# Three groups of transposes moved from TensorE to VectorE and swapped loads, and a silu as one ScalarE instruction, in a three-layer float32 model

## The reference, cut to what matters

```python
# even layer, short-convolution branch
y_a = sc_b * causal_depthwise_conv(sc_c * sc_v, sc_conv_w)
y_a = y_a * jax.nn.silu(sc_z)
# even layer, scan branch
xbc = jax.nn.silu(causal_depthwise_conv(ssd_xbc, ssd_conv_w) + ssd_conv_b)
xs, bm, cm = _split(xbc, (SSD_WIDTH, SSD_GROUPS * SSD_STATE, SSD_GROUPS * SSD_STATE))
y_b = ssd_chunked(xs, dt, a, bm, cm) + xs * ssd_d[:, None]
y_b = y_b.reshape(b_, l_, SSD_WIDTH) * jax.nn.silu(ssd_z)      # then a norm per group
return x + jnp.concatenate([y_a, y_b, y_m], axis=-1) @ w_out
# odd layer
y_c = causal_block_attention(q_full, k_full, v) * jax.nn.silu(z_c)
return x + jnp.concatenate([y_c, y_m], axis=-1) @ w_out
```

## Time and profile before

| what | us |
|---|---|
| median of 3 runs | 2671.36 |
| lowest and highest of them | 2669.19 and 2673.0 |
| the profiled execution's own time | 2667.36 |
| its span, first to last instruction | 2665.8 |
| TensorE busy in it | 2646.0 |
| VectorE busy | 1554.9 |
| ScalarE busy | 1348.1 |

### The profile page before, as it was taken

One profiled execution on the slowest core, in us unless ns is written; L12 is line 12 of the kernel. 1 busy time (PEld: TensorE's weight loads), 2 busy tenths in 40 slices (PEclk: granted clock), 3 DMA queues, 4 the chain that ended last, 5 costly groups with the idle time before them and its releaser, 6 DMA issues.

```text
span 2665.8 us, 35952 instructions
## 1 busy us (share of the span) xinstructions
PE 2646.0 (99%) x12095; PEld 2199.0 (82%) x12095; DVE 1554.9 (58%) x1827; ACT 1348.1 (51%) x1787; POOL 336.2 (13%) x519
## 2 busy tenths in 40 slices
PE   9999999999999999999999999999999999999998
PEld 7888888888888888888888878888888889888887
DVE  6444456667555555555454564446777765457864
ACT  6544455654444444444444554446565445555443
POOL 2100032211110000000000111001110010123300
PEclk9999999999999999999999999999999999999999
DMA  8866676678876767666666877666666777687664
GB/s 313 307 227 216 215 235 222 204 242 271 243 231 211 221 211 225 209 220 229 215 219 218 257 228 233 209 204 238 224 227 227 242 243 226 222 269 218 182 216 162
DMA packets 171057, 608.53 MB, mean 228 GB/s; under 512 B 22880, under 2 KB 22928, under 8 KB 170192
## 3 DMA queue, kind: packets, MB, share of 16 engines
q1 hardware_dynamic: 133632, 485.03, 55.3%
q0 software_dynamic: 36608, 121.07, 14.9%
q10 hardware_dynamic: 720, 1.11, 0.1%
HBM read 557.79 MB, written 50.90 MB: 228 GB/s over the span
## 4 chain that ended last, share of the span: by engine, by line
PE 92%; DVE 2%; issue 2%; DMA 2%; ACT 1%; POOL 0%; POOLq 0%; SPq 0%; ACTq 0%; DVEq 0%
PE acc L802 58%; PE acc L808 29%; DVE w_lo L1848 1%; DMA d_x<-tile 1%; DMA raw<-stream 1%; DMA r_b<-d_x 1%; PE turn L1098 1%; ACT w_hi L1285 0%; PE ps_s L1228 0%; PE ps_s L1229 0%; POOL r_b L558 0%; PE ps_y L893 0%; PE ps_y L1003 0%; PE ps_s L880 0%; PE ps_s L988 0%
## 5 line engine op out<-in xcount | busy, mean ns | idle before, releaser
L1848 DVE TENSOR_TENSOR w_lo<-raw,w_hi 128x1024 fp32r<-128x1024 f32 x919 | 1117.7, 1223 | 883.0 <-ACT w_hi L1285 876.3
L1285 ACT ACTIVATE w_hi<-raw 128x1024 fp32r<-128x1024 f32 x919 | 963.9, 1059 | 899.8 <-PE acc L808 821.9
L802 PE MATMUL acc<-w_hi,x_t_hi 128*128 128x512 f32 (+1 forms) x2400 | 950.5, 396 | 3.8 <-DVE x_t_lo L1897 3.1
L802 PE MATMUL acc<-w_hi,x_t_lo 128*128 128x512 f32 (+1 forms) x2400 | 933.5, 389 | 0.0
L808 PE MATMUL acc<-w_lo,x_t_hi 128*128 128x512 f32 (+1 forms) x2400 | 640.8, 389 | 0.2 <-DVE w_lo L1848 0.2
L802 PEld LDWEIGHTS acc<-w_hi,x_t_hi 128*128 128x128 f32 x2400 | 451.2, 188 | 96.2 <-DVE x_t_lo L1897 3.5
L808 PEld LDWEIGHTS acc<-w_lo,x_t_hi 128*128 128x128 f32 x2400 | 451.1, 188 | 93.1 <-DVE w_lo L1848 0.6
L802 PEld LDWEIGHTS acc<-w_hi,x_t_lo 128*128 128x128 f32 x2400 | 451.3, 188 | 90.5 <-issue 1.9
L802 PE MATMUL acc<-w_hi,ff_t_hi 128*128 128x512 f32 x352 | 136.9, 389 | 0.0
L802 PE MATMUL acc<-w_hi,ff_t_lo 128*128 128x512 f32 x352 | 136.9, 389 | 0.0
L808 PE MATMUL acc<-w_lo,ff_t_hi 128*128 128x512 f32 x352 | 94.1, 389 | 0.0
(11 more groups left out here) (398 smaller groups left out, 2691.9 us busy)
## 6 DMA issues: line engine op xcount, KB each, us to landing
raw<-stream SPq DMA_DIRECT2D x919, 512.0 KB, 4.3
d_in<-tile POOLq DMA_DIRECT2D x20, 512.0 KB, 3.8
d_ev<-tile POOLq DMA_DIRECT2D x20, 512.0 KB, 4.9
d_x<-tile POOLq DMA_DIRECT2D x16, 512.0 KB, 4.2
r_b<-d_x POOLq DMA_DIRECT2D x64, 128.0 KB, 5.9
xin<-d_x POOLq DMA_DIRECT2D x16, 512.0 KB, 8.6
d_h<-tile POOLq DMA_DIRECT2D x14, 512.0 KB, 5.0
h_b<-d_h POOLq DMA_DIRECT2D x56, 128.0 KB, 4.8
```

Of the source, the lines that this page charges most:

```text
L802: nc.tensor.matmul(out, src[x][:, chunk + c, t * P:(t + 1) * P], w_hi[:, s, w], start=first and c == 0 and x == 0, stop=False)
L1285: nc.scalar.activation(w_hi[:, u.slot, :], raw[:, u.slot, :], ACT.Copy).then_inc(hi_ready, 1)
L1848: nc.vector.tensor_tensor(w_lo[:, s, :], raw[:, s, :], w_hi[:, s, :].bitcast(F32), ALU.subtract).then_inc(lo_ready, 1)
```

## The change

RES_AT of the stage "gate" goes from (8, 9, 10) to (7, 8, 9). The scan's 768 columns are loaded by four swapped loads into `u_b` and transposed by one VectorE instruction into `u_t` in SBUF, at position 15 of the group before; the convolution reads `u_t`. The silu of the convolution and that of the gate become one ScalarE instruction each, both at position 4, and VectorE's multiplies go. The short convolution's halves are loaded swapped, and its two operands are transposed by VectorE; the halves stand 9 positions apart, and TensorE waits for the second before unit 22. Tiles 0 to 2 of the latent output are written to `d_h` and read back swapped through ScalarE's DMA queue, transposed by VectorE and split by `high_blocks` and `low_blocks`; tile 3 stays as it was. The columns are put in order on the host. GpSimd's loads of `xin` for the last residual wait for the third of these tiles, since they share its memory.

```diff
-RES_AT = {"mix": (5, 6, 8), "ffo": (5, 6, 7), "gate": (8, 9, 10)}
+RES_AT = {"mix": (5, 6, 8), "ffo": (5, 6, 7), "gate": (7, 8, 9)}
```

GpSimd's queue, the loads for the scan and the short convolution, and the wait ahead of the last residual's loads:

```diff
         def load_u(g):
-            pool.dma_start(u_in[:, :, 0:512], ev_v[:, :, bass.ds(g.times(512, 1024), 512)]).then_inc(s_u, 16)
-            for m in range(2):
-                pool.dma_start(u_in[:, :, 512 + m * P:640 + m * P],
-                               ev_v[:, :, bass.ds(g.times(P, 3072 + 512 * m), P)]).then_inc(s_u, 16)
+            for b in range(P // SQ):
+                w = 1024 + 768 * g.k + 6 * SQ * b
+                pool.dma_start(u_b[b * SQ:(b + 1) * SQ, :, :],
+                               d_ev[:, w:w + 6 * SQ].rearrange("(a j) n -> j a n", j=SQ)).then_inc(s_u, 16)
...
-            for t in range(TH):
-                pool.dma_start(sc_in[:, t, :, :].rearrange("p a n -> p (a n)"),
-                               ev_v[:, t, 6144 + 2048 * j:6144 + 2048 * (j + 1)]).then_inc(c_in, 16)
+            for b in range(P // SQ):
+                w = 6144 + 2048 * j + NBW * b
+                pool.dma_start(sc_in[b * SQ:(b + 1) * SQ, :, :, :].rearrange("p a k n -> p a (k n)"),
+                               d_ev[:, w:w + NBW].rearrange("(a j) n -> j a n", j=SQ)).then_inc(c_in, 16)
...
+        pool.wait_ge(turn_lo, 2 * (TURN["oy"] + 3) + 2)
         for b in range(4):
             free = [] if b < 2 else [(sums_out, B0["oout"] + b + 1)]
             load_tile(halves(d_x4), At(b), b % 2, free)
```

TensorE, scan (the transposes at position 0):

```diff
-            if p == 0:
-                pe.wait_ge(s_u, n.times(48, 48))
+            if p == 7:
                 pe.wait_ge(dt_v, 7)
                 pe.wait_ge(s_yb, n.times(1, 1))
-                for c in range(6):
-                    bank = (turn[0], turn[1], ps_s)[c // 2]
-                    for t in range(TH):
-                        mm = nc.tensor.transpose(bank[:, (c % 2 * TH + t) * P:(c % 2 * TH + t + 1) * P],
-                                                 u_in[:, t, c * P:(c + 1) * P], ident[:, :])
-                mm.then_inc(s_ut, 1)
-            if p == 7:
```

TensorE, beside eout (its function `short`, with 2 x 16 transposes, is removed):

```diff
-            if q == 20:
-                pe.wait_ge(c_lo, 2)
+            if q in (20, 22):
+                pe.wait_ge(c_lo, q // 2 - 9)
```

TensorE, latent output:

```diff
-            for n in range(4):
+            for n in range(3, 4):
                 for h in range(2):
                     if p == GATED + 8 * n + 2 * h:
```

ScalarE, scan:

```diff
             if p == 4:
                 act.wait_ge(s_conv, n.times(3, 3))
-                nc.scalar.activation(th[:, :], cv[:, :, :].rearrange("p c t -> p (c t)"), ACT.Tanh)\
-                    .then_inc(s_th, 1)
-            if p == 5:
+                c_ = cv[:, :, :].rearrange("p c t -> p (c t)")
+                nc.scalar.activation(c_, c_, ACT.Silu, scale=2.0).then_inc(s_silu, 1)
                 act.wait_ge(s_z, n.times(16, 16))
-                nc.scalar.activation(zth[:, :, :], zt[:, :, :], ACT.Tanh, scale=0.5).then_inc(s_zth, 1)
+                nc.scalar.activation(zt[:, :, :], zt[:, :, :], ACT.Silu).then_inc(s_zs, 1)
```

ScalarE, latent output (tile 3 keeps the steps of before):

```diff
+            for n in range(3):
+                if p == GATED + 8 * n - 1:
+                    act.wait_ge(l_tile, n + 1)
+                    act.dma_start(halves(d_h), ybuf[:, :, n * NBW:(n + 1) * NBW]).then_inc(heads_in, 16)
+                if p == GATED + 8 * n + 1:
+                    act.wait_ge(heads_in, OUT_MOVES * n + 16)
+                    if n:
+                        act.wait_ge(turned, 2 * (TURN["oy"] + n))
+                    for b in range(P // SQ):
+                        act.dma_start(o_b[b * SQ:(b + 1) * SQ, :, :],
+                                      d_h[:, b * P:(b + 1) * P].rearrange("(a j) n -> j a n", j=SQ)).then_inc(heads_in, 16)
+                if p == GATED + 8 * n + 5:
+                    high_blocks(TURN["oy"] + n, o_r, o_t, n)
```

VectorE, scan (the two multiplies at positions 5 and 6 are removed; this is called at position 15 of the stage ez and of groups 0 to 2):

```diff
+        def turn_u(g):
+            dve.wait_ge(s_u, 64 * (g + 1))
+            dve.wait_ge(s_conv, 3 * g)
+            nc.vector.transpose(u_t[:, :, :].rearrange("p c (a i) -> p c a i", i=SQ),
+                                u_b[:, :, :].rearrange("p a (c i) -> p c a i", i=SQ)).then_inc(s_ut, 1)
```

VectorE, short convolution (its steps stand at positions 9j + 4, 6, 7, 8, 9 and 11, where they stood at 7j + 4, 6, 8 and 11):

```diff
+            for at, src, dst, ready, done in ((6, 1, sc_u, c_u, c_ut), (7, 0, sc_w, c_w, c_wt)):
+                if k == 9 * j + at:
+                    dve.wait_ge(ready, j + 1)
+                    dve.wait_ge(c_y, j)
+                    nc.vector.transpose(dst[:, :, :].rearrange("p c (a i) -> p c a i", i=SQ),
+                                        sc_in[:, :, src, :].rearrange("p a (c i) -> p c a i", i=SQ)).then_inc(done, 1)
```

VectorE, latent output:

```diff
+                if n < 3 and p == GATED + 8 * n + 4:
+                    turn_blocks(TURN["oy"] + n, OUT_MOVES * (n + 1), o_b, o_r, heads_in)
+                if n < 3 and p == GATED + 8 * n + 7:
+                    low_blocks(TURN["oy"] + n, o_r, o_t, n)
```

More of the change, by code:

```diff
@@ L244, in program @@
     lat_junk = place("lat_junk", [P, 2560], F32, XT + 3 * K)
+    o_b = place("o_b", [P, TOK // SQ, P], F32, END + 8 * K)
+    o_r = place("o_r", [P, 4 * TOK], F32, END + 12 * K)
     zgt = place("zgt", [P, TH, NBW], F32, WD + 64 * K)
@@ L1122, in _ @@
             pair_of("sc", 2 * g, 0, 0, 8, x3_t, 0, lambda p: sc_beside(p, g))
-        def short(p, j):
-            if p == 8 + 7 * j:
-                if j:
-                    pe.wait_ge(c_y, j)
-                else:
-                    pe.wait_ge(turn_lo, 2 * TURN["x4"] + 2)
-                pe.wait_ge(c_u, j + 1)
-                pe.wait_ge(c_w, j + 1)
-                for src, banks, s_ in ((sc_in[:, :, 1, :], turn, c_ut), (sc_in[:, :, 0, :], (ps_s, ps_y), c_wt)):
-                    for h in range(2):
-                        for c in range(2):
-                            for t in range(TH):
-                                mm = nc.tensor.transpose(
-                                    banks[h][:, (c * TH + t) * P:(c * TH + t + 1) * P],
-                                    src[:, t, (2 * h + c) * P:(2 * h + c + 1) * P], ident[:, :])
-                        mm.then_inc(s_, 1)
         for q, (b, k) in enumerate(EOUT_ORDER):
@@ L1145, in _ @@
             turn_group(q, 3)
-            for j in range(2):
-                short(q, j)
             if q == 6:
@@ L2383, in sc_beside @@
                 low_group(p, g - 1)
+            if p == 15 and g < 3:
+                turn_u(g + 1)
         for g in range(4):
@@ L2598, in latent_heads @@
                     for t in range(TH):
-                        last = nc.vector.tensor_scalar(ybuf[:, t, J * P:(J + 1) * P],
-                                                       ps_y[:, t * P:(t + 1) * P], sums[:, 4 + t:5 + t], None,
-                                                       ALU.mult)
+                        y_ = ybuf[:, t, J // 4 * NBW:(J // 4 + 1) * NBW].rearrange("p (b c i) -> p b c i", b=4, i=SQ)
+                        y_ = y_[:, :, J % 4, :] if J < 12 else ybuf[:, t, J * P:(J + 1) * P]
+                        z_ = ps_y[:, t * P:(t + 1) * P]
+                        last = nc.vector.tensor_scalar(y_, z_.rearrange("p (b i) -> p b i", i=SQ) if J < 12 else z_,
+                                                       sums[:, 4 + t:5 + t], None, ALU.mult)
                     last.then_inc(l_y, 1)
@@ L2702 @@
     w0 = a["w_in0_2"]
-    ein = np.concatenate([w0[:, 9248:EVW], w0[:, 6144:9216], w0[:, 4096:6144]], axis=1)
+    xbc = np.concatenate([w0[:, 6144:8192].reshape(D, 4, 4, 4, SQ)] + [
+        w0[:, at:at + 512].reshape(D, 4, 1, 4, SQ) for at in (8192, 8704)], axis=2).transpose(0, 1, 3, 2, 4)
+    ein = np.concatenate([w0[:, 9248:EVW], xbc.reshape(D, -1), w0[:, 4096:6144]], axis=1)
     dt = w0[:, 9216:9248].reshape(16, P, 32).transpose(1, 0, 2).reshape(1, P, -1)
-    short = np.concatenate([w0[:, 1024 * m + NBW * j:1024 * m + NBW * (j + 1)]
-                            for j in range(2) for m in range(4)], axis=1)
+    short = w0[:, :4096].reshape(D, 4, 2, 4, 4, SQ).transpose(0, 2, 4, 1, 3, 5).reshape(D, -1)
     out0 = np.concatenate([a["w_out0_2"][1024:], a["w_out0_2"][:1024]])
```

73 lines of the change are left out of this document (33 added, 40 removed).

## The result

The changed kernel takes 2672.18 us (median of 20 runs, 2667.70 to 2676.46), the kernel before takes 2668.11 us in the same session (20 runs, 2665.05 to 2673.00). The ratio is 1.0013, 95% interval 1.0007 to 1.0019. That is a slowdown of about 0.1%, inside what I had called no change, and 17.5 us above the forecast of 2654.7. The forecast stood on a median of 3 runs, 2671.36, which is 3.2 us above that of the 20: measured on the change alone, 16.7 us were to be won and 4.1 were lost.

The account below looks back on a forecast made before the run. TensorE bounds the kernel, busy 2646.0 of 2665.8 us. Gains 5.40 + 3.54 + 2.76 + 5.01 = 16.7 us take 2667.36 to 2650.7, plus 4.0 for the median gives 2654.7 us; range 2650 to 2663.

Parts of the forecast that it names:

- the cover: Whole change: added work fits into idle time and leads on the other engines and transfers, without making TensorE wait.
- Gate: Opening of ein: TensorE's wait for the residual's low part goes, winning 5.01 us, with 0.7 us in hand.
- Latent output: Four transposes fewer at each of six places win 2.76 us; the added stores, loads and transposes cost nothing.
- Scan: Twelve transposes fewer per group, 1.35 us each group, win 5.40 us over four groups.
- So it has a little less to do than before: VectorE in a scan group: gains a transpose of 1.86 us, loses a 1.75 us multiply and another of 1024 columns.
- 2.6 us are left: Scan position 4: ScalarE's split of unit 7 ends at 1910.8, TensorE wants it at 1913.4.
- Rival (4): Scan position 4: ScalarE late behind two table loads and two silu, each group waits 5.0 us, 2674.7 us; chance 0.03.
- The table loads cost no time: Scan: two loads a group, 2.56 us, fit into ScalarE's 3.72 us idle before the silu.
- a late load would first eat the ring's lead: Scan operands: even a late swapped load would first use the lead of the splits queued on VectorE; landing takes 5.9 us.
- Short convolution: Sixteen transposes fewer per half, 1.77 us each half, win 3.54 us over two halves.
- four loads for two: Short convolution: GpSimd issues four swapped loads where it issued two; no cost was put on them.
- The closing test of the prediction: Whole kernel: the prediction is wrong if TensorE's idle time grows by more than it loses.

Follow-up runs that it names:

- turn10: The changed kernel with VectorE's transpose of the scan's operands at position 10 of the group before (12 in ez), not 15; ratio 1.0005.
- scan2: The changed kernel with VectorE's transpose at position 10, first tap on VectorE, other taps moved, load sent early, z_t_hi before silu, z's silu at 5; ratio 0.9958.
- scan2_tanh: scan2 with tanh and VectorE's multiply in place of the scan's silu; ratio 0.9951.
- load_early: The changed kernel with GpSimd's load of the next group's operands sent once VectorE has turned the last ones, not behind the silu; ratio 0.9998.

## Why the prediction was wrong

Two terms of the sum were right and two weren't. The step that failed is the cover: that what was added, and what came earlier, had room on the other engines and in the transfers.

**Gate: right.** The order of VectorE's steps came as worked out; only the reserve was 1.75 us for 0.7. **Latent output: right**, also in that it costs nothing. A position with the tile now takes as much as one without, 2468.03 less 2464.55 = 3.48 us for 3.93 and 3.47 in the earlier trace rows:

```profile
2464.55 0.49 PE L1214 MATMUL turn<-ident,lp 128*128 128x128 f32 x3
2468.03 1.08 PE L815 MATMUL acc<-w_lo,x_t_hi 128*128 128x512 f32 x4
```

**Scan: what was removed was priced rightly**: over position 0 of the second group the distance after is 1892.25 less 1889.53 = 2.72 us, as forecast. The 5.40 us were lost, and 10.80 more, because the cover fails at four places of the text.

- "So it has a little less to do than before" of VectorE was true of the group and false of its positions. What it loses stands at 5 and 6, what it gets stands at 15, ahead of three positions in which it already needs 3.5 us for TensorE's 2.72. turn10 bought 3.4 us back. The transpose itself was sized well, 1.77 us for 1.86.
- "2.6 us are left" was worked out for unit 7, by the earlier trace rows. The nearest thing in that queue was not a split but z_t_hi, and behind it z_t_lo, with 0.46 us. Both effects on it, 1.35 us less of transposes and 1.04 us of silu ahead, were in my own text, 4.07 less 2.72 for the one and "the gate's silu of 1.05 us" for the other; the reader of them was not. Three waits came of it, 1.35 - 0.46 + 1.04 = 1.93 by this sum and 1.84 to 1.87 in the trace, and each cost TensorE 2.32 us. Rival (4) named the place (position 4, ScalarE late) and had the chance of 0.03. Its point of decision was taken at the wrong reader.
- "The table loads cost no time": the loads are there, 7 in the scan, and as such they cost at most the 1.6 us of scan2 against scan2_tanh. In the changed kernel, though, silu was 8 us dearer than tanh (scan +10.80 against +2.86). load_early, with silu, takes back 6.3 of it by the load alone; what part of tanh's advantage is the same 6.3 wasn't tried apart.
- "a late load would first eat the ring's lead" looked at a load that comes late. I never asked what it does to the others when it leaves early. I had read GpSimd's queue for its four issues and not for the semaphore in front of them.

The Trainium skill's figure of a drain of about 1.38 us with a table switch ("ScalarE: Activation LUTs", section "What ACT_TABLE_LOAD costs") isn't borne out: in scan2's rows above the exponential starts 0.01 us behind the end of the load, and the load is issued 0.02 us or so behind the instruction before it; all 7 loads of the scan in the changed kernel took 1.28 us. The whole switch is 1.3 us of ScalarE there.

**Short convolution: the term was 3.54 us, the measure is +0.41.** The step that failed is the cost of GpSimd's "four loads for two", of which I counted the issues and not the pieces. Unswapped, 3.26 of the 3.54 are there, with VectorE's added work in place: that cover was judged rightly.

The closing test of the prediction, that TensorE's idle time grows by more than it loses, is what came: 7.8 us less of work and 10.6 us more of idle time.

## What to carry to other kernels

An edit that takes work off the bounding engine brings every later appointment forward by what it takes: list each reader within one period of the loop with its reserve (here 0.46 us at one of them, on a gain of 1.35), not only the one nearest the edit. Ask of each chain that ends there whether the edit brings it forward as well. Count the load of a helping engine position by position, and look at what each signal that comes earlier sets free, above all transfers that then meet a refilling ring. Price a swapped load by its pieces: compare the GB/s that the transfer engines move at a full share, not the number of issues.

## What the runs showed that I had not expected

- Small pieces fill the transfer engines without moving much: 253 and 247 GB/s for 376 at a share of 0.98 to 0.99, over the 16 us from the issue, where 1024 pieces of 2 KB stand for 256 of 8 KB in a 2 MB load.
- Weights sent beside one swapped load of 768 KB take nearly twice as long to land (8.8 us, and 4.7 for the weights of the same stretch with the load moved away). Moving it by one semaphore took 6.3 us off the scan, making it one unswapped load 2.5 us.
- A table load runs in 1.28 us with no drain in sight, and silu over 1536 columns takes as long as tanh (1.49 us each). Silu and the exponential load a table each time they take turns (2 loads in each of groups 2 to 4); the tanh behind the last silu, at 2069.7, had no load.
